# Three of nine expert tiles summed from a streamed V table instead of gathered V rows

## What is computed

```python
def peer_block(h, peer_wq, peer_keys, peer_u, peer_v):
    '''h: (n, D). Product-key retrieval over N_KEYS^2 single-neuron experts, PEER_HEADS heads.'''
    ...
    sc, ix = lax.top_k(s, PEER_TOPK)
    ...
    eid = jnp.take_along_axis(cid, pos, axis=-1)
    g = jax.nn.softmax(top, axis=-1)
    act = jax.nn.gelu(jnp.einsum('nhkd,nd->nhk', peer_u[eid], h).astype(jnp.float32))
    w = (g * act).astype(h.dtype)
    return jnp.einsum('nhk,nhkd->nd', w, peer_v[eid])
```

## Time and profile before

| | us |
|---|---|
| timed executions, median of 3 | 4452.92 |
| their range | 4448.04 to 4454.62 |
| the profiled execution, first to last instruction (span) | 4610.3 |

### The profile page before, as it was taken

One profiled execution on the slowest core, in us unless ns is written; L12 is line 12 of the kernel. 1 busy time (PEld: TensorE's weight loads), 2 busy tenths in 40 slices (PEclk: granted clock), 3 DMA queues, 4 the chain that ended last, 5 costly groups with the idle time before them and its releaser, 6 DMA issues.

```text
span 4610.3 us, 46291 instructions
## 1 busy us (share of the span) xinstructions
PE 3486.6 (76%) x16122; PEld 1731.9 (38%) x16122; DVE 2734.5 (59%) x6463; ACT 911.3 (20%) x1858; POOL 2441.7 (53%) x2375
## 2 busy tenths in 40 slices
PE   7989999989899898978898988998443344433456
PEld 4656755655356443544443554434100000000011
DVE  3443412788876768775568757777843565575410
ACT  3552310134423100133444222001000000000000
POOL 0000000275777565567776766655666666666665
PEclk9999999999999899999999988998655555555567
DMA  7774452799999999999998999999999899999998
GB/s 305 285 263 191 163 164 82 277 328 329 347 377 374 384 419 400 407 351 378 391 387 321 375 358 406 407 403 393 374 378 379 336 372 377 374 370 352 375 372 316
DMA packets 422693, 1572.17 MB, mean 341 GB/s; under 512 B 47720, under 2 KB 63464, under 8 KB 411328
## 3 DMA queue, kind: packets, MB, share of 16 engines
q0 software_dynamic: 340384, 1289.90, 72.2%
q1 hardware_dynamic: 78448, 271.38, 15.8%
q10 hardware_dynamic: 3632, 7.94, 0.5%
HBM read 1526.42 MB, written 42.61 MB: 340 GB/s over the span
## 4 chain that ended last, share of the span: by engine, by line
PE 42%; DVE 18%; POOL 11%; another core or an unknown queue 10%; issue 9%; DMA 8%; ACT 1%; ACTq 0%; DVEq 0%; SPq 0%; POOLq 0%
PE bank L2606 7%; DVE peer_u_ring L2712 6%; PE wide L1891 6%; DMA peer_v_ring<-in_peer_v,expertsT 5%; POOL peer_u_ring L2539 4%; PE wide L1460 4%; PE wide L808 4%; POOL peer_v_ring L2549 4%; PE wide L2233 4%; PE wide L1448 3%; PE wide L871 2%; POOL w_ring L2549 2%; DMA peer_u_ring<-in_peer_u,experts 2%; PE wide L881 2%
## 5 line engine op out<-in xcount | busy, mean ns | idle before, releaser
L2539 POOL DMA_INDIRECT peer_u_ring<-in_peer_u,experts x1098 | 1153.2, 1050 | 603.0 <-issue 299.5
L2549 POOL DMA_INDIRECT peer_v_ring<-in_peer_v,expertsT x840 | 881.9, 1050 | 515.1 <-PE bank L2606 222.6
L2712 DVE SCALAR_TENSOR_TENSOR peer_u_ring<-peer_u_ring,wide 128x1024 f32<-128x1024 f32 x654 | 781.7, 1217 | 408.0 <-DMA peer_u_ring<-in_peer_u,experts 325.8
L2606 PE MATMUL bank<-peer_v_ring,peer_lone 128*32 128x512 f32 x3360 | 607.6, 730 | 450.3 <-DMA peer_v_ring<-in_peer_v,expertsT 280.9
L2606 PE MATMUL bank<-w_ring,peer_lone 128*32 128x512 f32 x1056 | 303.5, 962 | 345.7 <-DMA w_ring<-in_peer_v,expertsT 199.5
L2712 DVE SCALAR_TENSOR_TENSOR peer_u_ring<-peer_u_ring,peer_h 128x1024 f32<-128x1024 f32 x444 | 532.4, 1219 | 15.0 <-DMA peer_u_ring<-in_peer_u,experts 9.9
L2606 PEld LDWEIGHTS bank<-peer_v_ring,peer_lone 128*32 128x32 f32 x3360 | 92.8, 117 | 791.3 <-issue 771.9
L2549 POOL DMA_INDIRECT w_ring<-in_peer_v,expertsT x264 | 252.3, 956 | 141.2 <-issue 74.6
L808 PE MATMUL wide<-hT,w_ring 128*128 128x384 f32 x768 | 271.5, 501 | 6.9 <-ACT hT L589 3.6
L2606 PEld LDWEIGHTS bank<-w_ring,peer_lone 128*32 128x32 f32 x1056 | 50.5, 140 | 582.0 <-issue 576.6
L1460 PE MATMUL wide<-w_ring,hT 128*128 128x256 f32 x1152 | 260.4, 383 | 0.2 <-issue 0.2
(11 more groups left out here) (332 smaller groups left out, 5204.5 us busy)
## 6 DMA issues: line engine op xcount, KB each, us to landing
w_ring<-in_weights SPq DMA_DIRECT2D x312, 512.0 KB
sb_kc<-in_kcT POOLq DMA_DIRECT2D x16, 2048.0 KB, 7.7
sb_vc<-in_vc POOLq DMA_DIRECT2D x16, 2048.0 KB, 8.6
peer_u_ring<-in_peer_u,experts POOLq DMA_INDIRECT x1098
mod_w<-in_w_ada SPq DMA_DIRECT2D x15, 1024.0 KB, 10.8
peer_v_ring<-in_peer_v,expertsT POOLq DMA_INDIRECT x840
mod_w_later<-in_w_ada SPq DMA_DIRECT2D x9, 1024.0 KB, 7.0
scores<-sel_sc SPq DMA_DIRECT2D x6, 1024.0 KB
```

The lines of the kernel that those rows point to most:

```text
L2539: pool.indirect_dma_start(buffer, None, K.A["peer_u"], bass.IndirectOffsetOnAxis(ap=K.ids_of[:, j % CHOSEN, k:k + 1], axis=0)).then_inc(lo ...
L2549: pool.indirect_dma_start(buffer, None, K.A["peer_v"], bass.IndirectOffsetOnAxis(ap=K.ids_of_turned[:, j % CHOSEN, t:t + 1], axis=0)).then ...
L2606: last = pe.matmul(self.F.psum[strip:strip + 32, :], self.lone[:, mark - at:mark - at + 32], self.buffer("v", m)[0][:, c * HALF:(c + 1) * ...
L2712: dve.scalar_tensor_tensor(u, u, 1.0, h2, ALU.mult, ALU.mult, accum_out=self.dots[:, j % 2, k:k + 1]).then_inc(self.dot_done, 1)
```

## The change

The second group's three tiles (`DENSE`: j = 3, 4, 5) fetch no V rows. Their experts' numbers and weights are kept (`dense_ids`, `dense_w`). When the stages are over, for each token the weight of expert (row r, column c) is spread into a matrix: DVE compares the row key and the column key of each of the 128 slots with a ramp 0..127, which gives two one-hot matrices, multiplies the row one with the weights (`place`), and PE multiplies the two (`build`), 8 tokens a batch. ACT copies the batch from PSUM into `dense_wT`. Rows are taken in three passes (0 to 42, 43 to 85, 86 to 127). Behind each pass's 48 batches the V table's chunks of that pass (128 rows of the table each, loaded in order by the sync engine's queue, SP, into 5 buffers) are multiplied with the matrix, for three tiles and two halves of the channels, and added up in six PSUM banks (`add_block`).

These units form a third stream. It starts at slot 756 and its last sum stands at slot 1223; `slots()` spreads the units by weight, 2.0 for a batch and 5.1 for a chunk, over slots that count 1 where only U or only V is fetched and 2 where both are. That puts the batches at slots 758 to 830, 949 to 985 and 1070 to 1106, and the chunks' sums between and behind them. The three tiles are ended after the sums (slots 1232 to 1248).

Slots of tiles 0, 4, 5 and 6 now fetch U rows alone (`lone`), and those of tiles 4 and 5 that lie beside stages count 0.8 in `paces()`. The V ring keeps 6 buffers to tile 7, 14 for tile 8. The rings of experts' numbers and gates hold 2 tiles instead of 4 (`CHOSEN`). `by_banks` is false from slot 768 on. Everything before slot 370 keeps its place.

```diff
-CHOSEN = 4
+CHOSEN = 2
...
+DENSE = range(GROUPS[1].first, GROUPS[1].first + GROUPS[1].nt)
+FETCHED = [j for j in range(TILES) if j not in DENSE]
+def lone(j):
+    return j == 0 or j - 1 in DENSE
...
-        weights = [LONE_U if s < SLOTS else 1.0 for s in range(before, to)]
+        weights = [LONE_U if lone(s // SLOTS) else 1.0 for s in range(before, to)]
...
-        return not any(self.K.leave_banks(G) <= s < self.K.take_banks(G) for G in GROUPS[1:])
+        return s < SLOTS * GROUPS[-1].first and not any(self.K.leave_banks(G) <= s < self.K.take_banks(G) for G in GROUPS[1:])
...
-            if 0 <= j < TILES:
+            if j in FETCHED:
                 for i in range(P // 2):
                     if self.value_slot(i) == k:
                         fetch_v(j, 2 * i)
                         fetch_v(j, 2 * i + 1)
...
+class Dense:
+    PASSES, BATCH, CHUNK_BUFFERS = ((0, 43), (43, 86), (86, P)), 8, 5
+    FROM, UNTIL, END_EVERY = SLOTS * GROUPS[-1].first - MARGIN + 2, SLOTS * TILES + 72, 8
+    SHARED = range(SLOTS * GROUPS[-1].first + 14, SLOTS * (GROUPS[-1].first + 1) - 4)
+    BUILD, SUM = 2.0, 5.1
...
+    def slots(self):
+        weights = [1.0 if lone(s // SLOTS) or s >= SLOTS * TILES else 2.0 for s in range(self.FROM, self.UNTIL)]
+        total = sum(self.BUILD if u[0] == "build" else self.SUM for u in self.units)
...
+    def build(self, pe, n, t, at):
+        shared = b % 2 and self.slot_of[self.units.index(("build", n, t, at))] in self.SHARED
+        bank = self.bank_of[key] = K.banks[7 if shared else 4]
+        out = bank.begin(pe, key)
+        pe.wait_ge(self.placed, 3 * (b + 1))
+        for i in range(self.BATCH):
+            last = pe.matmul(out[:, i * (hi - lo):(i + 1) * (hi - lo)], self.col[:, b % 2, i, :], self.row[:, b % 2, i, 0:hi - lo], start=True, stop=True)
...
+    def add_block(self, pe, n, i):
+        pe.wait_ge(*self.landed(i))
+        for t in range(len(DENSE)):
+            for c in range(2):
+                last = pe.matmul(bank.psum, self.wT[:, i - lo, t, :], v[:, c * HALF:(c + 1) * HALF], start=(i == 0), stop=(i == P - 1))
...
+    def place(self, dve, n, t, at):
+        if b >= 2:
+            dve.wait_ge(self.bank_of[key].full, self.bank_of[key].full_at[key])
+        dve.tensor_tensor(row, self.ramp[:, lo:hi].unsqueeze(1).broadcast_to([P, self.BATCH, hi - lo]),
+                          self.row_of[:, t, these].unsqueeze(2).broadcast_to([P, self.BATCH, hi - lo]), ALU.is_equal).then_inc(self.placed, 1)
+        dve.tensor_tensor(col, self.ramp[:, :].unsqueeze(1).broadcast_to([P, self.BATCH, P]),
+                          self.col_of[:, t, these].unsqueeze(2).broadcast_to([P, self.BATCH, P]), ALU.is_equal).then_inc(self.placed, 1)
+        dve.tensor_tensor(row, row, self.K.dense_w[:, t, these].unsqueeze(2).broadcast_to([P, self.BATCH, hi - lo]), ALU.mult).then_inc(self.placed, 1)
```

More of the change, by code:

```diff
@@ L2449, in F, with issues @@
         return self.K.banks[7]
-    def places(self):
-        more = self.K.NW
-        users = [[] for _ in range(NU + NV + more)]
-        for n in range(SLOTS * TILES):
-            users[n % (NU + NV) if n < SLOTS else (n + self.TURN) % NU].append(("u", n))
-        for m in range(P * TILES):
-            users[NU + m % NV if m < P * self.MORE_FROM else NU + m % (NV + more) if m < P * (TILES - 1) else (m + NU) % (NU + NV + more)].append(("v", m))
-        return {who: (r, n + 1, had[n - 1] if n else None) for r, had in enumerate(users) for n, who in enumerate(had)}
+    def issues(self):
+        for s in range(-AHEAD, SLOTS * (TILES + 1)):
+            if s + AHEAD < SLOTS * TILES:
+                yield "u", s + AHEAD
+            j, k = (s + AHEAD - 1) // SLOTS - 1, (s + AHEAD - 1) % SLOTS
+            if j in FETCHED:
+                for i in range(P // 2):
+                    if self.value_slot(i) == k:
+                        yield "v", self.row(j, 2 * i)
+                        yield "v", self.row(j, 2 * i + 1)
+    def places(self):
+        place, counts, held = {}, [0] * (NU + NV), [None] * (NU + NV)
+        u, v, alone = 0, 0, True
+        for kind, n in self.issues():
+            if kind == "u":
+                if lone(n // SLOTS) != alone:
+                    alone = not alone
+                    u = u % NU if alone or (u - 1) % (NU + NV) < NU else 0
+                r = u % (NU + NV if alone else NU)
+                u += 1
+            elif n < P * (len(FETCHED) - 1):
+                r = NU + v % NV
+                v += 1
+            else:
+                if n == P * (len(FETCHED) - 1):
+                    v %= NV
+                r = (NU + v) % (NU + NV)
+                v += 1
+            counts[r] += 1
+            place[kind, n] = r, counts[r], held[r]
+            held[r] = kind, n
+        return place
     def buffer(self, kind, n):
@@ L2496, in g2_loads @@
     def g2_loads(self, j):
-        out, kind = 0, None
-        for t in ORDER[:j + 1]:
+        out, kind = 1, None
+        for t in [ORDER[n] for n in FETCHED if n <= j]:
             if (t == PTILES) != kind:
@@ L2517, in load_g2 @@
         def load_g2(j):
[L2518 removed]
+            if j and self.g2_loads(j) == self.g2_loads(j - 1):
                 return
@@ L2616, in tensor @@
     def tensor(self, pe):
+        dense = Beside(self.K.dense.tensor(pe))
         for s in range(SLOTS * (TILES + 1)):
@@ L2624, in tensor @@
                 for i in range(P // 2):
-                    if self.value_slot(i) == k:
+                    if j in FETCHED and self.value_slot(i) == k:
                         self.add_values(pe, j, i)
+            dense.upto(self.K.dense.due(s))
             yield
@@ L2664, in scalar @@
     def scalar(self, act):
+        dense = Beside(self.K.dense.scalar(act))
         for s in range(SLOTS * (TILES + 1) + self.SUMS_AT + 1):
@@ L2669, in scalar @@
             turned = False
-            if j >= 0:
-                if k == 0 and j < TILES:
+            if 0 <= j < TILES:
+                if k == 0:
                     self.gelu(act, j)
                     turned = True
-                if j < TILES:
-                    if k == self.WEIGH_AT + 3:
-                        self.keep_turned(act, j)
-                        self.set_alone(act, j, 0)
-                        self.set_alone(act, j, 1)
-                    for r in range(2, 8):
-                        if k == self.value_slot(8 * (r - 1)) + 5:
-                            self.set_alone(act, j, r)
-                    if k == self.value_slot(31) + 1:
-                        self.keep_sums(act, j, 0)
-            if j >= 1 and k == self.SUMS_AT:
+                if k == self.WEIGH_AT + 3:
+                    self.keep_turned(act, j)
+            if j in FETCHED:
+                if k == self.WEIGH_AT + 3:
+                    self.set_alone(act, j, 0)
+                    self.set_alone(act, j, 1)
+                for r in range(2, 8):
+                    if k == self.value_slot(8 * (r - 1)) + 5:
+                        self.set_alone(act, j, r)
+                if k == self.value_slot(31) + 1:
+                    self.keep_sums(act, j, 0)
+            if j - 1 in FETCHED and k == self.SUMS_AT:
                 self.keep_sums(act, j - 1, 1)
+            dense.upto(self.K.dense.due(s))
             yield turned
@@ L2751, in vector @@
     def vector(self, dve):
+        dense = Beside(self.K.dense.vector(dve))
         for s in range(SLOTS * (TILES + 2)):
@@ L2784, in stream_layer_kernel @@
         K.peer = peer = Peer(K)
+        K.dense = dense = Dense(K)
         stages = (norm, stick, gla, mix, res, select)
@@ L2840, in _ @@
                         stage.sync(sp, G)
+                dense.sync(sp)
                 peer.sync(sp)
```

267 lines of the change are left out of this document (218 added, 49 removed).

## The result

The changed kernel takes 4659.66 us (median of 4, 4654.38 to 4667.18) against 4453.77 us for the kernel before, timed beside it (median of 4, 4448.04 to 4463.85): a ratio of 1.046, 95% interval 1.044 to 1.048, or +206 us. The forecast was 4510 us with a range of 4385 to 4620. The sign was right, the size and the range were not.

The account below looks back on a forecast made before the run. No single engine bounds the kernel; each stretch has its own fullest engine or transfers. Stages -161 and +219 behind them sum to +58 us on the profiled 4610.3, scaled to +56: 4510 us, range 4385 to 4620.

Parts of the forecast that it names:

- scaled, +56: 4510: Whole kernel: +58 us on the profiled 4610.3, scaled by 0.966 to the timed 4452.9, giving +56 and 4510 us.
- batches bound by DVE, +120: 75 V slots with 96 batches: DVE 313 us busy, at 0.92 340 us against 220, +120 (ends +93, +150).
- The other batch stretch, slots 754 to 831: 48 batches there: DVE 202 us busy, at 0.92 219 us, +26 (ends +9, +34).
- Sum slots: 181 V slots with sums: 3.5 us each, 634 us against 511, +123 (ends +90, +159).
- Rival 3: Batch slots: PE waits for DVE and drops to its lower clock; 4710 us, 4610 if half comes; chance 0.10.
- h2 in SBUF, costed at nothing: Dots reading h2 from SBUF: POOL gathers 1.10 instead of 0.95 us, two 2.8 us, under the 3.5 us slot.
- The stages were to gain 161 us: Stages, slots 370 to 753: +55 and -216 give -161 us, ending at about 3117 us.
- slots 370 to 511: First part of the stages: 461 us of PE at a fill of 0.91, 506 us against 451, +55.
- the lone slots: Slots 512 to 753: PE and DVE busy times over 1.79 give 622 us against 838, -216.
- signs of being wrong: Lone slots under 2.3 us, sum slots staying near 3 us, or a clock near 0.5 in batch slots.
- Rival 2: Faster: every stretch runs at its fullest engine with no gap; -119, 4338 us, half way 4425; chance 0.34.
- Rival 4: V slots: POOL's gathers wait for whole dots, 4.9 us a slot, 4755 us, from 1.45 us a gather; chance 0.03.

Follow-up runs that it names:

- experiment 1: The kernel before, unchanged, profiled a second time: 4451.3 us, with a span of 4449.5 us.
- Experiment 9: The changed kernel with batches in bf16, weights split into a bf16 part and a bf16 rest, both multiplied: 4567.67 us, ratio 1.026.
- experiment 6: The kernel before with one line of the change, dots reading h2 from SBUF from slot 768 on: 4495.17 us, ratio 1.009.
- experiment 4: The changed kernel without its batches (matrix zero) and with only 2 of the table's 128 chunks: 4246.97 us, ratio 0.953.
- experiment 7: The kernel before with the V ring kept at 6 buffers to tile 7 and 14 for tile 8: 4452.26 us, ratio 1.000.
- number 10: The changed kernel with two dense tiles (3 and 4), passes of 64 rows, four matmuls a chunk, h2 in PSUM: 4528.49 us, ratio 1.017.

## Why the prediction was wrong

**The step that failed in the number: the base.** The terms were worked out against the first profile and the sum was "scaled, +56: 4510". That takes the whole of the kernel, added work too, to be 3.4% shorter in a timed execution. The stages were hardly shorter (slots 370 to 753: 1289 us in the earlier trace rows, 1277 in experiment 1), and the V slots behind them were, by a tenth (slots 896 to 1150: 2.87 to 2.58 us each). These are the ones that wait for transfers: in experiment 1 DVE waits 215.9 us of these 659 for U gathers. The added engine work did not shrink. My absolute slot times, left as they were, make it plain: behind slot 754 the prediction has 219 + 115 + 634 + 340 + 153 + 91 = 1552 us, and the changed kernel took 1547. Experiment 1 shows 1196 there, so that against the right base the same terms are +356 - 161 = +195, or 4648 us, and 4660 with the stages' times taken whole as well (506 + 622 = 1128 against 1277). Either lies outside the range: the base is nearly all of the 150 us missed. I had named this ("transfer-bound stretches shrink and the added engine work does not") and used it for leaning, not in the sum.

**The step that failed in the mechanism: batches bound by DVE, +120.** I wrote for the 75 V slots with batches that "DVE is the bound here, since PE needs 2.05 + 0.6 with the copy", 340 us. They took 452. DVE's placing took what I gave it, 2.07 us a batch (1.22 + 0.51 + 0.51, less the overlaps). PE's side was priced from a row of stage matmuls at the full clock (0.128 us a record), and at the full clock the price was right: 1.88 to 1.98 us. But from 20 us into each of the two stretches the batches ran at 1.2 GHz, at 3.64 us and 0.55 more for the bank. The term is 112 us too small. Experiment 9, which makes PE's part cheap and DVE's dearer, takes 51 and 48 us off these two stretches: PE is what holds them. At the full clock 48 batches, 22 pairs of V rows at 1.07 us and the 11 us of sums in the second stretch would be some 130 us of PE, an estimate from these rows, less than DVE's 154: the bound that I had named. The other batch stretch, slots 754 to 831, was held by DVE as forecast (187.76 us busy of 192), and took 192 us, not 219.

**What hid it.** Sum slots were given 3.5 us, 634 in all; they took 3.1 us, 562. The PE work was as forecast within 5% (265.45/84 = 3.16 us, not 3.3), but PE had no gap at all, where I had put tile 0's 0.92. These two errors, +112 and -72, and the smaller ones of the other stretches (-27, -8, -10) nearly cancel in the 1552. That the sum behind the stages came out within 5 us is luck.

**Rival 3 came true, but not by its own mechanism.** It gave 4.1 + 0.6 us a batch, "270 us in each of two stretches instead of 170", 4710 us, and 4610 if half of it comes; measured were 226 and 225, and 4660. It let the clock fall because PE would idle about a quarter of the time. The rows show 7% idle, nearly all of it in waits of 0.55 us for the bank, and a granted clock of 0.54 to 0.55. The Trainium skill's account of a falling clock that the prediction leans on (TensorE: Matmul & The Clock Gate, "HAM oscillation — how this bites in real kernels") is about waits for transfers, longer than the bursts of matmuls between them. It is not "exactly" this case: these stretches have no such waits, so that account doesn't explain their clock. Rival 3's chance of 0.10 was too low: behind the stages the clock stood near 0.5 in every row until 4407.

**h2 in SBUF, costed at nothing.** I compared 2.8 us on POOL with a slot of 3.5 us. That holds beside the dense work (3.1 us a slot in the end). In the kernel before it costs 42 us (experiment 6), and the slots of experiment 4, where the dense work is gone, are as slow: 2.78 us.

**What held, in part by luck.** The stages were to gain 161 us and gained 147, and they ended at 3106 to 3118 us, as said. But the two halves were off by about as much each way: slots 370 to 511 took 464 us, not 506, since PE filled 0.94 of them and not 0.91; the lone slots took 666, not 622, since PE's and DVE's busy times add up to 1.71 times the span and not tile 0's 1.79. A chunk took the 5.4 us given, and sum slots ran at a clock of 0.95 to 0.98 with PE above 0.9. The smaller V ring cost the kernel before nothing (experiment 7); the ids' ring was not tried alone. Of the signs of being wrong that I had named, two came: sum slots at 3.1 us and a clock near 0.5 in batch slots, which took 6.0 us instead of 4.5. Rival 2 is out as a whole, since PE and DVE filled 0.82 and 0.89 of the lone slots, not 0.95; in the sum slots PE did run without a gap, as it says. Rival 4 is out: a U gather took POOL 1.06 to 1.37 us in the mean of a stretch, under its 1.45, and a sum slot 3.1 us, not 4.9.

**Is there a version that wins?** None of these. Three dense tiles have 206 us to spend and the dense work takes 413; in bf16 321 (4568 - 4247), with rounded weights 264. With two tiles transfers are the floor by a sum, not by a run: the table is 67 MB more than it saves behind the stages, 160 us at 419 GB/s, against 147 us won in the stages of the changed kernel (139 in number 10), so even free batches would end above 4452. Also not tried was a second bank for the batches of the second and third stretch; PE's idle time there, 15 to 16 us each, is the most that it could give by itself.

## What to carry to other kernels

Where the profile is longer than the timed runs, don't scale the sum: find the stretches that wait for transfers, take the difference off there, and leave added engine work whole. A matmul's price has to be read at the clock of the stretch where it will stand: here the row's price was right at the full clock and a little over half of it at the lower one. A change that moves work out of a full stretch into one that looks idle should be priced at that stretch's own clock and fullest engine first.
